# Two MLPs and two feed-forwards on one core: a reciprocal, a down block's end, form steps and weight splits placed elsewhere

## What is computed

```python
def rms_norm(x, g):
    return x * lax.rsqrt(jnp.mean(x * x, axis=-1, keepdims=True) + RMS_EPS) * g

def squared_relu_mlp(h, w_up, w_down):          # 1024 -> 4096 -> 1024, h is a normed x
    u = jax.nn.relu(h @ w_up)
    return (u * u) @ w_down

def swiglu_ffn(x, g, w_gate, w_up, w_down):     # 1024 -> 2816 -> 1024
    h = rms_norm_2(x, g)
    return (jax.nn.silu(h @ w_gate) * (h @ w_up)) @ w_down

# first_block:  h = h + mixer(...);  h = h + squared_relu_mlp(rms_norm(h, g_mlp[layer]), ...)   (2 layers)
# second_block: x = x + 0.5 * swiglu_ffn(...);  x = x + mixers;  x = x + 0.5 * swiglu_ffn(...)
```

## Time and profile before

| | us |
|---|---|
| median of 3 timed runs (2444.93 to 2446.68) | 2445.65 |
| the profiled execution | 2442.93 |
| its span | 2441.1 |
| TensorE busy | 2418.4 (99%) |
| VectorE busy | 1644.7 (67%) |
| ScalarE busy | 1186.3 (49%) |
| GpSimd busy | 153.3 (6%) |

### The profile page before, as it was taken

How to read it: one execution, slowest core, us unless ns; L and a number is a source line. 1 busy time by engine, 2 the same in 40 slices (tenths; PEclk the granted TensorE clock), 3 DMA queues, 4 the chain that set the end, 5 groups by cost and what they waited for, 6 DMA issues and landing times.

```text
span 2441.1 us, 36042 instructions
## 1 busy us (share of the span) xinstructions
PE 2418.4 (99%) x13644; PEld 2085.8 (85%) x13644; DVE 1644.7 (67%) x2437; ACT 1186.3 (49%) x1813; POOL 153.3 (6%) x143
## 2 busy tenths in 40 slices
PE   9999999999999999999999999999999999999999
PEld 7888789988888888789988889998787778789998
DVE  6777756666566555756656877666868846866664
ACT  3676535545334343535536544445465453544443
POOL 2000100001000000200002100002000001000000
PEclk9999999999999999999999999999999999999999
DMA  4111345542222222255532455552222213555552
GB/s 140 60 52 52 122 146 139 156 130 87 87 86 78 77 87 86 86 164 156 156 114 74 149 148 164 147 154 86 79 70 70 78 61 99 151 148 160 151 152 82
DMA packets 108195, 273.52 MB, mean 112 GB/s; under 512 B 15120, under 2 KB 33808, under 8 KB 107920
## 3 DMA queue, kind: packets, MB, share of 16 engines
q1 hardware_dynamic: 95168, 237.98, 29.0%
q0 software_dynamic: 8640, 31.46, 7.6%
q10 hardware_dynamic: 4240, 2.10, 0.3%
HBM read 269.40 MB, written 2.10 MB: 111 GB/s over the span
## 4 chain that ended last, share of the span: by engine, by line
PE 91%; DVE 5%; issue 2%; ACT 1%; POOL 1%; DMA 0%; DVEq 0%; ACTq 0%; SPq 0%; POOLq 0%
PE ps L2850 28%; PE ps L3171 16%; PE ps L2855 14%; PE ps L3175 8%; PE ps L3184 6%; PE ps L3251 4%; PE ps L3552 2%; PE ps L2919 2%; PE ps L3294 1%; PE ps L3074 1%; PE ps L2903 1%; PE ps L3031 1%; PE ps L3050 1%; PE ps L3015 1%; PE ps L3281 1%
## 5 line engine op out<-in xcount | busy, mean ns | idle before, releaser
L829 ACT ACTIVATE w_hi<-raw 128x1024 fp32r<-128x1024 f32 x286 | 302.3, 1059 | 763.0 <-PE ps L2855 577.1
L1680 DVE TENSOR_TENSOR w_lo<-raw,w_hi 128x1024 fp32r<-128x1024 f32 x286 | 352.4, 1232 | 118.6 <-ACT w_hi L829 118.3
L2850 PE MATMUL ps<-x_hi,w_hi 128*128 128x512 f32 x848 | 337.0, 397 | 4.6 <-DVE u_act L2057 4.3
L2850 PE MATMUL ps<-x_lo,w_hi 128*128 128x512 f32 x848 | 330.5, 390 | 0.0
L2850 PE MATMUL ps<-u_hi,w_hi 128*128 128x512 f32 x642 | 250.9, 391 | 2.8 <-ACT w_hi L829 2.8
L2850 PE MATMUL ps<-u_lo,w_hi 128*128 128x512 f32 x642 | 249.9, 389 | 0.0
L3171 PE MATMUL ps<-xs_hi,ring 128*128 128x256 f32 x960 | 240.8, 283 | 1.3 <-ACT second_copy L1040 1.3
L3171 PE MATMUL ps<-xs_lo,ring 128*128 128x256 f32 x960 | 240.7, 283 | 0.0
L1033 ACT ACTIVATE ring<-forms 128x512 fp32r<-128x512 f32 x300 | 187.7, 628 | 88.0 <-PE ps L3175 86.0
L2855 PE MATMUL ps<-x_hi,w_lo 128*128 128x512 f32 x848 | 209.5, 389 | 0.0
L2850 PEld LDWEIGHTS ps<-x_hi,w_hi 128*128 128x128 f32 x848 | 159.3, 188 | 43.6 <-issue 9.1
(11 more groups left out here) (495 smaller groups left out, 4769.6 us busy)
## 6 DMA issues: line engine op xcount, KB each, us to landing
raw<-in_stream SPq DMA_DIRECT2D x293, 512.0 KB, 3.3
forms<-in_stream SPq DMA_DIRECT2D x180, 256.0 KB, 4.3
forms<-in_stream SPq DMA_DIRECT2D x60, 512.0 KB, 4.5
forms<-in_stream POOLq DMA_DIRECT2D x60, 512.0 KB, 5.6
x_tok<-in_x SPq DMA_DIRECT2D x4, 512.0 KB, 7.5
out_x<-xn ACTq DMA_DIRECT2D x7, 256.0 KB, 2.3
tab_ret<-in_tables_ret SPq DMA_DIRECT2D x1, 1536.0 KB, 6.7
raw<-in_stream SPq DMA_DIRECT2D x3, 256.0 KB, 3.2
```

The costliest lines, as they stand in the source:

```text
L829: nc.scalar.activation(w_hi[:, slot(n)], raw[:, slot(n)], ACT.Copy).then_inc(hi_done, 1)
L1680: nc.vector.tensor_tensor(w_lo[:, slot(n)], raw[:, slot(n)], w_hi[:, slot(n)].bitcast(F32), ALU.subtract).then_inc(lo_done, 1)
L2850: nc.tensor.matmul(ps[:, gemm_bank(n)], w_hi[:, s, k], x(k), start=(k == 0 and i == 0), stop=False)
```

## The change

In words:
- MLPs, VectorE: `inverse(norm)` and inv_sq move from the turn of up block 0 to that of up block 5, behind its u_lo.
- Feed-forwards, TensorE: in each group n's last chunk (kc - 1) comes straight after n + 1's chunks 0 to 3, and n + 1's chunks 4 to kc - 1 follow in one part. The MLPs' order stays.
- Feed-forwards, VectorE: ahead of the pairs, form_low of the fourth unit and fourth_form move behind x_normed_low(0 to 2).
- Feed-forwards, ScalarE: x_normed_high(3) moves from unit (first pair, 6) to (first pair, 5), the first unit.
- Feed-forwards, ScalarE and VectorE: the splits of down blocks n and n + 1 move from (first pair, 3) and (second pair, 6) to (second pair, 6) and (third pair, 6).
- Feed-forwards, SP: in group 0 load_forms of the fourth pair (qs[1] + 2) moves ahead of the load of block n + 3.

```diff
@@ load_layer (SP)
                     load(n)
+                    if layer >= 2 and g == 0:
+                        load_forms(qs[1] + 2)
                     load(n + 1)
                     for q in qs:
-                        if q + 2 < PAIR_FROM[layer + 1] and (layer < 2 or g or q > qs[0]):
+                        if q + 2 < PAIR_FROM[layer + 1] and (layer < 2 or g or q > qs[1]):
                             load_forms(q + 2)
@@ gate_pairs (ScalarE)
-                    if g == 0 and (q, p) == (qs[0], 6):
+                    if g == 0 and (q, p) == (qs[0], 5):
                         x_normed_high(layer, 3)
@@ gate_pairs (ScalarE; the same on VectorE with split_lo)
-                    if g == 0 and (q, p) in ((qs[0], 3), (qs[1], 6)):
-                        split_hi(RUN_AT[LAYERS[layer]] + 2 * FFN_DENSE + q - qs[0])
+                    if g == 0 and (q, p) in ((qs[1], 6), (qs[2], 6)):
+                        split_hi(RUN_AT[LAYERS[layer]] + 2 * FFN_DENSE + q - qs[1])
@@ mlp (VectorE)
                     split_lo(n + 2)
-                    if c == 0:
-                        inverse(norm)
-                        nc.vector.tensor_tensor(inv_sq[:], inv[:], inv[:], ALU.mult).then_inc(flag("down_scaled"), 2)
                     dve.wait_ge(sig("uh_done"), chunks_before + c + 1)
                     nc.vector.tensor_tensor(u_lo[:, 0, c], u[:, c % 2], u_hi[:, 0, c].bitcast(F32),
                                             ALU.subtract).then_inc(sig("ul_done"), 1)
+                    if c == 5:
+                        inverse(norm)
+                        nc.vector.tensor_tensor(inv_sq[:], inv[:], inv[:], ALU.mult).then_inc(flag("down_scaled"), 2)
@@ ffn (VectorE)
                         third_form(PAIR_FROM[layer])
-                        form_low(v)
-                        form_low(v + 1)
-                        fourth_form(PAIR_FROM[layer])
-                        form_low(v + 2)
-                        form_low(v + 3)
+                        for i in range(3):
+                            form_low(v + i)
                         for i in range(3):
                             x_normed_low(layer, i)
+                        form_low(v + 3)
+                        fourth_form(PAIR_FROM[layer])
@@ up_and_down (TensorE)
                     down_part(n + 1, made, range(4), kc)
                     if layer < 2:
                         down_part(n, made, (kc - 2,), kc)
-                    else:
-                        down_part(n + 1, made, range(4, kc - 1), kc)
                     down_part(n, made, (kc - 1,), kc)
-                    down_part(n + 1, made, range(4 if layer < 2 else kc - 1, kc), kc)
+                    down_part(n + 1, made, range(4, kc), kc)
```

## The result

| | kernel before | changed kernel |
|---|---|---|
| median of the first comparison, us | 2445.61 | 2430.43 (2430.20 to 2431.07) |
| median beside it in a later set, us | 2445.14 | 2430.55 (2430.30 to 2431.43) |
| profiled execution, us | 2442.93 | 2430.65 |
| its span, us | 2441.1 | 2428.8 |

The ratio is 0.9938 with a 95% interval of 0.9921 to 0.9955 (in the later set 0.9940, 0.9926 to 0.9953). The change is faster, as predicted, and the profiled execution is 12.3 us shorter where 12.7 were summed. But the median fell by 15.2 us, and the range ended at 2430.9, 0.5 above it. The question for the experiments is where the other 2.9 us come from.

A forecast was written before the change was run, and what follows sets the result against it. TensorE, busy 2418.4 of 2441.1 us, bounds the kernel, so only its waits count. 4.86 + 3.36 + 1.13 + 2.16 + 1.2 = 12.7 us off 2445.65 gives 2432.95; range 2430.9 to 2437.0.

The forecast's parts named there:

- Part 1: Both MLPs: moving the reciprocal ends TensorE's wait for u_act ahead of block 4; 2.43 x 2 = 4.86 us.
- thin cover of block 8's weights: Second MLP: w_lo split ended 0.3 us before block 8 started; claimed the cover grows, cost zero, otherwise 2.1 us.
- Part 2: Both feed-forwards, order of first two down blocks: w_hi waits go; 3.36 us in groups 0 and 1, 1.13 in group 2.
- all 0.84 come back: Groups 0 and 1, both feed-forwards: n ends 2.72 us ahead, hand-over takes 1.62, so the 0.84 us lost returns; 3.36 together.
- VectorE's and ScalarE's steps behind n (eviction, split of n+2) only come sooner: Part 2, down blocks of the feed-forwards: claimed the steps following block n are never later after the reorder.
- Part 3: Feed-forwards, weight splits one pair later: second pair's wait for last_copy goes, 1.08 us per layer, 2.16 together; form loads zero.
- The forms' move: Part 3, SP queue: fourth pair's load_forms goes out at 1413 instead of behind 1414.55; VectorE's 1.35 us wait shrinks; zero gain.
- rival (d): Feed-forwards, SP queue: fourth pair's forms land late, past about 1.2 us free each us costs TensorE one; 2450.5; chance 0.03.
- Part 4: Start of feed-forward pairs: x_lo sooner, 1.0 to 1.1 us in the second; second_copy 0.1 in each layer; sum 1.2.
- I keep that distance: First paragraph: timed median 2445.65 lies 2.72 us above the profiled 2442.93; the same distance was carried to the forecast median.
- no part of a wait is clock: First paragraph: TensorE's mean granted clock is 1.000, so only what a matmul waited for counts.
- the rivals: (b) thin cover fails, about 2435.6, chance 0.14; (c) only part works, 2437.6, chance 0.11; (d) slower, chance 0.03.

The follow-up runs named there:

- the first comparison: Changed kernel, four executions, against the kernel before: median 2430.43 us for 2445.61, ratio 0.9938.
- a later set: Changed kernel as it is, five executions, run again beside the kernel before: 2430.55 us for 2445.14, ratio 0.9940.
- the kernel with part 2 alone: Kernel before with only the lines of the change in up_and_down (order of the first two down blocks): 2440.85 us, ratio 0.9981.
- the filling matmuls: Kernel before plus seven matmuls nobody reads ahead of block 4 of both MLPs, u_act wait kept: 2443.88 us, ratio 0.9993.
- the earlier load: Filled kernel plus the fourth pair's forms loaded one down block earlier on SP's queue in both feed-forwards: 2442.93 us, ratio 0.9990 against the kernel before.
- the first set of runs: First of three experiment sets, with 30 executions of the unchanged kernel beside it: median 2445.49 us, 2443.03 to 2449.26.

## Why the prediction was right, and where it was not

**Part 1: right in the profile.** 2.42 and 2.38 us for 2.43 each. In the changed kernel u_act of block 2 starts at 287.60 and block 4 at 288.99, the next 5.44 later:

```profile
287.60 0.69 DVE L2059 TENSOR_SCALAR u_act<-ps 128x512 f32<-128x512 f32 x1
...
288.99 0.39 PE L2851 MATMUL ps<-x_hi,w_hi 128*128 128x512 f32 x1
...
294.43 0.39 PE L2851 MATMUL ps<-x_hi,w_hi 128*128 128x512 f32 x1
```

The eviction was forecast at 287.35 in the time of before, and that execution runs 0.24 later from block 2 on: 287.59. The thin cover of block 8's weights in the second MLP held and grew, as argued:

```profile
1040.79 3.34 DVE L1717 RECIPROCAL inv<-std 128x512 f32<-128x512 f32 x1
1044.23 0.69 DVE L2066 TENSOR_TENSOR inv_sq<-inv 128x512 f32<-128x512 f32 x1
...
1045.44 1.21 DVE L1682 TENSOR_TENSOR w_lo<-raw,w_hi 128x1024 fp32r<-128x1024 f32 x1
```

w_lo is split 6.2 us sooner than at 1051.66. The first MLP accounts for 2.2 of that; the other 4.0 is more than the 2.9 that I had allowed the split and the loads behind it, and more than the 2.4 of TensorE, so the cover of 0.3 us grew by 1.6.

**Part 2: right, but for a wait of 0.2 us that it overlooked.** The step "all 0.84 come back" holds in group 1 and in the second feed-forward: in group 1 of the first, n + 2 starts at 1567.77, four plain matmuls (0.91) behind 1566.86, and the block behind it 5.44 later. It does not hold in group 0 of the first. TensorE in order of time, beside the earlier trace rows, then its weight loads, then VectorE:

```profile
1442.46 1.07 PE L3185 MATMUL ps<-u_hi,w_lo 128*128 128x512 f32 x4
1443.43 0.50 PE L2851 MATMUL ps<-u_hi,w_hi 128*128 128x512 f32 x1
1443.77 0.39 PE L2851 MATMUL ps<-u_lo,w_hi 128*128 128x512 f32 x1
...
1449.01 0.39 PE L2851 MATMUL ps<-u_hi,w_hi 128*128 128x512 f32 x1
...
1443.43 0.19 PEld L2851 LDWEIGHTS ps<-u_hi,w_hi 128*128 128x128 f32 x1 [0.32 <-DVE h L1862]
...
1438.51 3.35 DVE L1717 RECIPROCAL inv_final<-std_final 128x512 f32<-128x512 f32 x1
1441.90 0.75 DVE L1942 SCALAR_TENSOR_TENSOR h<-h,prm,inv_final 128x512 f32<-128x512 f32 x1
1442.68 0.69 DVE L1862 SCALAR_TENSOR_TENSOR h<-ps,h 128x512 f32<-128x512 f32 x1
```

From 1442.46 four matmuls take 0.91 and n + 2 starts after 0.97; its second matmul comes 0.34 later in place of 0.23, and the block behind it 5.58 later in place of 5.44. So 0.06 + 0.14 of the 0.84 stay. The list of TensorE's matmul waits does not name it, but the weight load ahead of n + 2 waits 0.32 us for VectorE: the eviction of block n (L1862) frees its bank only at 1443.37, since VectorE does another reciprocal first, that of the final norm, which only this group has. The w_hi that the prediction followed is ready 1.5 us earlier (its copy starts at 1440.85 and takes 1.06). "VectorE's and ScalarE's steps behind n (eviction, split of n+2) only come sooner" was the failed step of this part: n ends sooner, but VectorE is not free to take it out. The kernel with part 2 alone shows the same 0.97 (1452.15 to 1453.12). Group 2 starts 0.55 behind 1668.63 for 0.45, the "0.1 or less" of the forecast. The whole part measured 4.6 us alone, for 4.5.

**Part 3: right in its waits, undersized in typical executions.** last_copy of the second pair starts at 1409.90 and is done by 1410.32, its unit starts at 1410.84, and no unit of that pair waits. The forms' move was costed at zero. In the first profile it was zero; over many executions it is worth about 1 us, a gain that the prediction's own rival (d) held with its sign turned round. In the changed kernel GpSimd issues at 1415.04 and VectorE takes the sum at 1421.37 without waiting.

**Part 4: right.** 1.21 us for 1.0 to 1.1, and 0.10 for second_copy in the first feed-forward; in the second the 0.1 did not come (5.48 and 5.52 us from x_lo to second_copy).

**The step that failed** is the last line of its first paragraph: "the median of the timed runs, 2445.65, lies 2.72 above it, and I keep that distance". The distance was treated as a constant of measuring. It was work of the kernel: about 1.3 to 1.9 us from clocks lowered behind the wait that part 1 removes, and about 1 us from the form that part 3 brings sooner. In the changed kernel the profiled execution lies 0.2 above its median instead of 2.7 below. Both shares were taken out of the kernel before by other means, the filling matmuls and the earlier load, and its median was then 2442.93, with no distance left. The same paragraph's "no part of a wait is clock" is the other side of that step. The range gave the forecast 2 us downwards for rounding and spread, and the median came out 2.5 below it: 2.9 from the distance, less 0.4 by which the parts were summed too high.

None of the rivals happened. Of (d), the fourth pair's forms came sooner, not later, in each profile with the change's third part, and the group-1 forms behind them do arrive late (VectorE waits 2.58 us for them at 1433.92) without TensorE waiting, as costed.

## What to carry to other kernels

If the profiled execution is faster than every timed one, the difference can be work of the kernel: look for waits that are near their cover, and for stretches of lowered clock that a lucky execution was spared, before the gap is carried through a sum as a constant. A wait of TensorE of about 2 us cost another 1.5 to 1.9 in what followed it, in some executions only, so removing it is worth more than its length, and filling it with matmuls nobody reads brings back that part alone. The mean clock of each execution, listed beside its time, showed the first of the two in the first set of runs. And a cover has to be read in each place: here the same wait had 0.96 us left in one feed-forward and 0.4 in the other.

## What the runs showed of the hardware

- TensorE's clock fell to its lower level behind an idle time of 2.15 us, in an otherwise busy stretch, in 72 of 118 executions with two such places. In five stretches profiled it fell up to 1.5 us after work had started again and stayed for seven to eight matmuls of 128x512; one reads 3.37 us at 0.42 each for 1.8 at 0.23, and each block lost 1.55 to 1.6 us. With 1.28 us or less in that place it stayed at 1.000 in 44 of 44.
- A DMA that accumulates into a 128x1024 tile took 7.2 us from GpSimd's issue to the first use in one execution and 8.1 in another of the same program. With 0.4 us lost ahead of its issue, that is the difference between hidden and not.
- TensorE restarts slowly: the first matmul behind a wait is followed at 0.31 to 0.34 us, not 0.23. This holds too where only the weight load ahead of it waited (0.32 us for VectorE at 1443.43), which the list of matmul waits does not show.
